# Recurrence of a decoder layer: tables of two 64x64 diagonal blocks in place of 128x128 tables

## What is computed

```
def rwkv7_scan(state0, r, w, k, v, kk, a):
    def step(S, inp):
        r_t, w_t, k_t, v_t, kk_t, a_t = inp
        sa = jnp.einsum('bhvk,bhk->bhv', S, -kk_t)
        S = (S * w_t[:, :, None, :] + sa[..., None] * (kk_t * a_t)[:, :, None, :]
             + v_t[..., None] * k_t[:, :, None, :])
        return S, jnp.einsum('bhvk,bhk->bhv', S, r_t)
    ...
    S, out = lax.scan(step, state0, xs)
```

## Time and profile before

| | us |
|---|---|
| median of 3 runs | 2958.71 (2955.7 to 2959.27) |
| the profiled execution's span | 2956.9 |
| PE busy | 2724.3 (92%) |
| DVE busy | 1186.9 (40%) |
| POOL busy | 1230.9 (42%) |
| ACT busy | 527.8 (18%) |
| PE's share of the chain of work that ended last | 87% |
| scan, first pair product to the first instruction behind it | 1169.98 to 1592.21 |

### The profile page before, as it was taken

The page is one execution under the profiler, slowest core; times in us unless marked ns, Lnnn a source line. Parts: engine busy times, 40 slices in busy tenths (PEclk is TensorE's granted clock), DMA queues, the critical chain, the costliest instruction groups (busy, mean ns, idle before and its releaser), DMA issues.

```text
span 2956.9 us, 45589 instructions
## 1 busy us (share of the span) xinstructions
PE 2724.3 (92%) x17867; PEld 2604.0 (88%) x17867; DVE 1186.9 (40%) x2064; ACT 527.8 (18%) x1098; POOL 1230.9 (42%) x949
## 2 busy tenths in 40 slices
PE   5999999999999964988888798987999999999998
PEld 5999999999999962887876398986899999999997
DVE  6332233133614359556555553153353312331333
ACT  4110011011301012332324223012121100100112
POOL 4444444444544356423332446400444444444442
PEclk8999999999999986999998699998999999999999
DMA  3111111111321100000001214222211111111111
GB/s 108 46 46 47 47 48 47 46 46 41 109 61 44 41 31 0 1 1 1 1 1 68 97 47 121 92 86 86 91 45 46 46 48 48 47 46 46 46 38 73
DMA packets 220686, 150.24 MB, mean 51 GB/s; under 512 B 10831, under 2 KB 211113, under 8 KB 219946
## 3 DMA queue, kind: packets, MB, share of 16 engines
q1 hardware_dynamic: 217850, 135.11, 15.2%
q10 hardware_dynamic: 2256, 13.71, 1.2%
q0 software_dynamic: 480, 0.05, 0.0%
HBM read 134.80 MB, written 14.04 MB: 50 GB/s over the span
## 4 chain that ended last, share of the span: by engine, by line
PE 87%; DVE 7%; ACT 2%; issue 2%; DMA 0%; POOL 0%; SPq 0%; DVEq 0%; ACTq 0%; POOLq 0%
PE bank L372 24%; PE bank L374 23%; PE bank L373 23%; PE bank L1101 3%; PE bank L1107 2%; PE bank L1094 1%; PE bank L1539 1%; PE bank L1508 1%; PE bank L1572 1%; DVE TT L1014 1%; PE bank L1161 1%; PE bank L1132 1%; PE bank L1172 1%; DVE z L829 1%; PE bank L1173 0%
## 5 line engine op out<-in xcount | busy, mean ns | idle before, releaser
L345 POOL TENSOR_TENSOR w_hi<-raw,cst 128x512 fp32r<-128x512 f32 x366 | 464.2, 1268 | 1231.5 <-PE bank L374 1051.4
L372 PE MATMUL bank<-h_hi,w_lo 128*128 128x344 f32 x2856 | 915.4, 321 | 8.9 <-issue 7.5
L374 PE MATMUL bank<-h_hi,w_hi 128*128 128x344 f32 x2856 | 914.0, 320 | 0.0
L373 PE MATMUL bank<-h_lo,w_hi 128*128 128x344 f32 x2856 | 913.4, 320 | 0.0
L372 PEld LDWEIGHTS bank<-h_hi,w_lo 128*128 128x128 f32 x2856 | 536.0, 188 | 10.9 <-issue 9.2
L350 POOL TENSOR_TENSOR w_lo<-raw,w_hi 128x512 fp32r<-128x512 f32 (+1 forms) x398 | 514.1, 1292 | 64.7 <-ACT w_hi L342 35.0
L374 PEld LDWEIGHTS bank<-h_hi,w_hi 128*128 128x128 f32 x2856 | 536.7, 188 | 1.1
L373 PEld LDWEIGHTS bank<-h_lo,w_hi 128*128 128x128 f32 x2856 | 535.0, 187 | 1.4
L374 PE MATMUL bank<-hid_hi,w_hi 128*128 128x344 f32 x1056 | 337.8, 320 | 0.0
L372 PE MATMUL bank<-hid_hi,w_lo 128*128 128x344 f32 x1056 | 337.7, 320 | 0.0
L373 PE MATMUL bank<-hid_lo,w_hi 128*128 128x344 f32 x1056 | 337.6, 320 | 0.0
(11 more groups left out here) (312 smaller groups left out, 3459.4 us busy)
## 6 DMA issues: line engine op xcount, KB each, us to landing
raw<-in_ffn_gate SPq DMA_DIRECT2D x88, 256.0 KB, 2.9
raw<-in_ffn_up SPq DMA_DIRECT2D x88, 256.0 KB, 2.9
raw<-in_ffn_down SPq DMA_DIRECT2D x80, 256.0 KB, 2.7
raw<-in_w_in SPq DMA_DIRECT2D x44, 256.0 KB, 2.8
cache<-in_cache_mem_k SPq DMA_DIRECT2D x8, 1024.0 KB, 4.9
cache<-in_cache_mem_v SPq DMA_DIRECT2D x8, 1024.0 KB, 4.9
x_save<-x ACTq DMA_DIRECT2D x1, 4128.0 KB, 12.5
x<-x_save ACTq DMA_DIRECT2D x8, 516.0 KB, 6.8
```

Source lines behind the costliest of these rows:

```text
L345: nc.gpsimd.tensor_tensor(w_hi[part], raw[part], cst[:, C_ONE:C_ONE + 1, 0:ph["width"]].to_broadcast([P, nk, ph["width"]]), ALU.mult)\
L372: nc.tensor.matmul(out, b, hi, start=first, stop=False)
L373: nc.tensor.matmul(out, a, lo, start=False, stop=False)
L374: m = nc.tensor.matmul(out, a, hi, start=False, stop=last)
```

## The change

The tables keep only the two diagonal blocks. A table of one head is now 128 partitions by 64 columns: the block of chunk 0 on partitions 0 to 63, the block of chunk 1 on 64 to 127. In detail:

- *Pair*: 32 products of 64x64 outputs and 128 columns, in place of 16 of 128 outputs and 256 columns.
- *Levels*: flip is a plain product with the identity in place of a transpose. Flip, Y and delta are each 16 products of 64x64 with 64 columns, chunk 0 and chunk 1 in turn. The tables are grouped by head parity, q = 0 and 1, four heads each: two groups in place of four. Each level has one POOL instruction for LoT in place of two, two buffers for it, and four of DVE and two of ACT in place of eight and four, of the same size each.
- TT's base is one multiplication with a mask and two additions of the identity, one per chunk, each for q = 0 and 1. MQ (MT and QKT in one) is masked in two instructions.
- *State part*: the products X, U, state and so on are issued for all heads in one go, with one eviction of 512 columns in place of two of 256. The products with MQ and LQ contract 64 rows in place of 128. Each chunk's outputs have a bank of their own.
- Bt, Kt, Vt, TT, LQ, MQ and decm have two buffers. The rounds stay in sequence on PE (`scan_tensor`).
- The next round's inputs are made inside the level loop: BK and exd between levels 0 and 1, A in level 2, R in level 3, their exponentials on ACT between its copies. rates_vector(1) moves ahead of the scan, rates_vector(2) behind the first flip of round 0.
- The mask constants are packed anew: C_PAIR holds the strict and the inclusive triangle side by side, and two levels share a table.

The core of the diff. What it leaves out are the renamed constants, the buffer addresses, and the helpers whose body is one instruction moved as it was:

```diff
...
         NLV = LEVELS - 1
...
+        B_XU, B_ST, B_OUT, B_T = 0, 1, 2, 4
...
+        def pair_tensor(pe, m):
+
+            pe.wait_ge(S("tok_ev"), 3 * m + 3)
+            pe.wait_ge(S("R_made"), m + 1)
+            for side in (0, 1):
+                for ht in range(4):
+                    for hp in (0, 1):
+                        r = rows(hp)
+                        for ck in (0, 1):
+                            t = rows(ck)
+                            i = nc.tensor.matmul(
+                                bank[B_T + 2 * side + hp][t, ht * P:(ht + 1) * P].rearrange(
+                                    "p (a t) -> p a t", a=2),
+                                BK[r, side, ht, t], AR[m % 2][r, :, ht, t], start=True, stop=True)
+                        if ht == 3:
+                            i.then_inc(S("pair"), 1)
...
+        def y_tensor(pe, m, lv):
+            pe.wait_ge(S("Loff_masked"), NLV * m + lv + 1)
+            for q in (0, 1):
+                pe.wait_ge(S("T_flip_ev"), 2 * (NLV * m + lv) + q + 1)
+                for ht in range(4):
+                    for ck in (0, 1):
+                        t = rows(ck)
+                        i = nc.tensor.matmul(y_bank(lv, q)[t, ht * CH:(ht + 1) * CH],
+                                             LoT[lv % 2][t, q, ht, :], Ti[t, q, ht, :],
+                                             start=True, stop=True)
+                i.then_inc(S("Y_t"), 1)
...
+        def x_tensor(pe, n, ck):
...
+            for ht in range(4):
+                nc.tensor.matmul(bank[B_XU][t, ht * P:(ht + 1) * P], AR[n % 2][:, 0, ht, t],
+                                 st_T[:, e % 3, ht, :], start=True, stop=False)
+                for hp in (0, 1):
+                    hc = head_cols(hp, ht)
+                    i = nc.tensor.matmul(bank[B_XU][t, hc], MQ[n % 2][t, hp, ht, 0, :], Vt[n % 2][t, hc],
+                                         start=False, stop=hp == 1)
+            i.then_inc(S("X_t"), 1)
...
+        def scan_tensor(pe):
+            for n in range(8):
+                turn_tensor(pe, n)
+                pair_tensor(pe, n)
+                for lv in range(NLV):
+                    flip_tensor(pe, n, lv)
+                    y_tensor(pe, n, lv)
+                    delta_tensor(pe, n, lv)
+                for ck in (0, 1):
+                    x_tensor(pe, n, ck)
+                    out_state_tensor(pe, n, ck)
+                    out_v_tensor(pe, n, ck)
+                    u_tensor(pe, n, ck)
+                    state_tensor(pe, n, ck)
+                    out_u_tensor(pe, n, ck)
...
+        def base_vector(dve, m, q):
+            tt = TT[m % 2][:, q]
...
+            link(nc.vector.tensor_tensor(tt, LQ[m % 2][:, q, :, 0, :],
+                                         level_mask(0).to_broadcast([P, 4, CH]), ALU.mult))
             for ck in (0, 1):
...
+                i = nc.vector.tensor_tensor(tt[t], tt[t], cst[t, C_ID:C_ID + 1, t].to_broadcast([64, 4, CH]),
+                                            ALU.add)
+            i.then_inc(S("T_base"), 1)
...
+        def scan_vector(dve):
...
+            for n in range(8):
+                tok_vector(dve, n)
+                base_vector(dve, n, 0)
+                mq_vector(dve, n)
+                base_vector(dve, n, 1)
+                flip_vector(dve, n, 0)
+                if n == 0:
+                    rates_vector(2)
+                delta_vector(dve, n, 0)
+                if n < 7:
+                    grow_vector(dve, n + 1)
+                    before_vector(dve, n + 1)
...
```

More of the change, by code:

```diff
@@ L1061, in chunk_tensor, with chunk, rows, head_cols @@
-        def chunk_tensor(pe, n):
-            mmul = nc.tensor.matmul
-            heads = lambda q: [(j, (4 * q + j) // 2, (4 * q + j) % 2) for j in range(4)]
-            pe.wait_ge(S("BK_made"), 2 * n + 2)
-            pe.wait_ge(S("out_ev"), 2 * n)
-            pe.wait_ge(S("state_add"), 4 * n)
+        B_XU, B_ST, B_OUT, B_T = 0, 1, 2, 4
+        def chunk(n):
+            return slice(n * P, (n + 1) * P)
+        def rows(ck):
+            return slice(64 * ck, 64 * ck + 64)
+        def head_cols(hp, ht):
+            return slice((2 * ht + hp) * 64, (2 * ht + hp + 1) * 64)
@@ new lines, in delta_tensor @@
+        def delta_tensor(pe, m, lv):
+            for q in (0, 1):
+                pe.wait_ge(S("Y_ev"), 2 * (NLV * m + lv) + q + 1)
+                for ht in range(4):
+                    for ck in (0, 1):
+                        t = rows(ck)
+                        i = nc.tensor.matmul(flip_bank(lv, q)[t, ht * CH:(ht + 1) * CH],
+                                             Yl[t, q, ht, :], TT[m % 2][t, q, ht, :],
+                                             start=True, stop=True)
+                i.then_inc(S("D_t"), 1)
@@ new lines, in out_state_tensor, with out_v_tensor @@
+        def out_state_tensor(pe, n, ck):
+            t, e = rows(ck), 2 * n + ck
+            pe.wait_ge(S("out_ev"), max(e - 1, 0))
+            for ht in range(4):
+                nc.tensor.matmul(bank[B_OUT + ck][:, ht * CH:(ht + 1) * CH], st_T[:, e % 3, ht, :],
+                                 AR[n % 2][:, 1, ht, t], start=ht == 0, stop=False,
+                                 skip_group_check=True)
+        def out_v_tensor(pe, n, ck):
+            t = rows(ck)
+            for ht in range(4):
+                for hp in (0, 1):
+                    nc.tensor.matmul(bank[B_OUT + ck][rows(hp), ht * CH:(ht + 1) * CH],
+                                     Vt[n % 2][t, head_cols(hp, ht)], MQ[n % 2][t, hp, ht, 1, :],
+                                     start=False, stop=False, skip_group_check=True)
@@ new lines, in out_u_tensor @@
+        def out_u_tensor(pe, n, ck):
+            t = rows(ck)
+            pe.wait_ge(S("QB_masked"), n + 1)
+            pe.wait_ge(S("U_ev"), 2 * n + ck + 1)
+            for ht in range(4):
+                for hp in (0, 1):
+                    i = nc.tensor.matmul(bank[B_OUT + ck][rows(hp), ht * CH:(ht + 1) * CH],
+                                         Us[t, head_cols(hp, ht)], LQ[n % 2][t, hp, ht, 1, :],
+                                         start=False, stop=True, skip_group_check=True)
+            i.then_inc(S("out_t"), 1)
@@ L1832, in _ @@
             g.wait_ge(S("mix_p"), 35)
-            for n in range(8):
-                chunk_pool(g, n)
+            scan_pool(g)
             sample_pool(g)
@@ L1885, in _ @@
             prep_tensor(pe)
-            for n in range(8):
-                chunk_tensor(pe, n)
+            scan_tensor(pe)
             post_tensor(pe)
@@ L1942, in _ @@
             prep_scalar(act)
-            for n in range(8):
-                chunk_scalar(act, n)
+            scan_scalar(act)
             post_scalar(act)
@@ L1988, in _ @@
             prep_vector(dve)
-            for n in range(8):
-                chunk_vector(dve, n)
+            scan_vector(dve)
             post_vector(dve)
```

536 lines of the change are left out of this document (250 added, 286 removed).

## The result

| | before | after |
|---|---|---|
| median of the runs, us | 2958.4 | 2999.47 (2998.56 to 3001.41) |
| ratio, with its 95% interval | | 1.0144 (1.013 to 1.0159) |
| span of the profiled execution, us | 2956.9 | 2997.7 |
| first X of round 0 | 1207.21 | 1198.00 |
| first X of round 7 | 1577.09 | 1608.42 |

The change makes the kernel 41 us slower, where 26 us faster was forecast. The table says where: the start of the scan is 9.2 us earlier, seven rounds take 40.5 us more, and the end, from the last round's X on, takes 25.9 us in place of 15.1. These give +42.1; what stands behind the scan is 1.3 shorter, and the span is 40.8 longer.

A forecast was written before the change was run, and what follows sets the result against it. PE bounds the recurrence's levels: 4.75 us each, no idle. A round of 49.4 against 52.84 saves 24.1 over seven, the start saves 9.0, the end loses 7.4: 25.7 saved, 2933 us, range 2891 to 2973.

The forecast's parts named there:

- the hole before the levels: Between pair and first Y, PE mostly waits while DVE works; the clock then halves for 6.8 us, adding 1.6 us.
- The clock stays low: Rival: half clock persists through three levels and the doubled state products, +15 us a round, 3050 us; chance 0.04.
- the bonus products: Four DVE products of 1.2 us in the last round, where BK stood; they cost 2.5 us.
- Diagonal tiles work at once: Level products alternating between the two diagonal 64x64 tiles overlap: 29 ns a record, 3.6 us a level.
- 5.6 for the rival: Rival: diagonal tiles take turns at 58 ns a record, 5.6 us a level, +10 a round, 3013 us; chance 0.12.
- Changes of shape: In X, each tile shape change costs 0.14 us, eight changes instead of one: +1.0, X issued in 2.8 us.
- X to X': State part, from the first chunk's X to the next X: 9.95 us, with single evictions, addition and decay of 512.
- X to pair: Whole state part, from X to the next pair: 21.2 us against 17.2, a loss of 4.0.
- pair to Y: From pair products to the first Y: 8.5 us against 10.8, or 6.3 without POOL blocking DVE.
- first level: First level, lengthened by DVE making next inputs: 5.2 us, plus 1.6 for half clock, 6.8.
- DVE beside POOL: Between pair and first Y, DVE instructions reading only SBUF stall while POOL works; without blocking 6.3 us, not 8.5.
- a second level at the low clock: Upper-bound term: half clock covers another level after the hole, +2.0 us a round.

The follow-up runs named there:

- fill_u: Changed kernel with three unread 128x128 products filling PE's wait behind U, twice a round, other waits left; 2989.4 us, ratio 1.0109.
- fill_small: Changed kernel with PE's waits behind U, behind first out_u and between turn and pair filled by unread 64x64 products; 2928.8 us, ratio 0.9899.
- xgroup: Changed kernel with X's four AR products issued before its eight MQ products, so tile shape changes twice, not eight times; 2985.3 us, ratio 1.0092.
- halves: Changed kernel with X, U and the state's change again issued, evicted, added and decayed in halves of 256 columns; 2918.4 us, ratio 0.9873.
- fill_out: Changed kernel with four unread 128x128 products behind the first chunk's out_u only; 2995.3 us, ratio 1.0131.
- xwide: Changed kernel with X's MQ products contracting all 128 rows, not 64, so rows don't change shape (output wrong); 2957.1 us, ratio 1.0003.
- before_merge: Kernel before, large tables kept, with only X, U and state's change merged to one eviction, addition and decay, out_v ahead of U; 3034.5 us, ratio 1.0256.

## Why the prediction was wrong

**The one step that failed is the clock.** The forecast had it fall once a round, in the hole before the levels, for 6.8 us. It falls earlier as well, in the state part of the first chunk, and in four of the seven rounds it stays low until past the hole: 34 us a round at the low level. The prediction had the waits that do it, "Us is one eviction of 512, 0.6, and nothing lies beside it" and the decay behind which X starts, and priced them as time only. The first of them is enough in the change; with it filled, the second does it (fill_u). The rival *The clock stays low* is the case that came. It was given 0.04, on the argument that PE would be full again at half speed. It looked at the wrong place: the levels do bring the clock back, and most of the low stretch lies ahead of them. Nor does a full PE bring it back at once: between 1206.7 and 1230.5 PE is busy for 21.25 of 23.80 us. The rival's price was +15 us a round; the whole measured excess over the forecast's round, 58.63 less 49.4, is 9.2. The 27 us added at half speed would cost half of that, 13.6, if PE alone set the pace (an estimate); the waits for DVE and ACT within them take no longer, so it is less.

Set against the sum: first X 1198.0, forecast 1198.2. Rounds 410.4, forecast 7 x 49.4 and 2.5 for the bonus products, 348.3: +62.1. End 25.9, forecast 20.0: +5.9. The first X is 0.2 early, and what stands behind the scan 1.3 shorter: the span 2997.7 is 66.5 above the forecast's 2931.2. In fill_small, where only the waits are filled, the same marks stand at 1196.5, 350.2 and 19.6 (1546.63 to 1566.27, where the scan ends), the forecast's end of the scan being 1198.2 + 348.3 + 20.0 = 1566.5. It takes 2929 us for a forecast of 2933. That two kernels of different time agree with one sum doesn't make the prediction right; it shows that the clock in the state part is the one large term at fault. That the two ends agree to 0.2 us is partly luck: the start is 1.7 us early, the rounds are 1.9 late, and the stages below are off by up to 0.4 us a round, some up and some down.

**Diagonal tiles work at once: right.** The level's period is 3.66 (1242.29 to 1245.95), forecast 3.6 and 5.6 for the rival. The rule of the Trainium skill (TensorEngine Tiling (Array Packing), Restrictions and Gotchas), which taken literally forbids the pair, is not borne out: flip, Y and delta write 64x64 tiles of different rows and columns into one bank, 32 records in 1.15 us, 0.22 of it the tail, 29 ns each. Pair even has four tiles at once, 64 records of 128 columns in 1.98 with the tail, 28 ns each; the forecast kept this as a bound.

**Changes of shape: right.** X is issued in 2.94 us (1198.00 to 1200.94), forecast 2.8; xgroup gives 0.15 for a change (14.2 us in 96, a part of them at half speed). The Trainium skill says, in the same page's Tiling Modes, that a change of mode drains TensorE; the trace agrees and prices it.

**The stages with the waits filled**, from fill_small, where the clock is low only in and behind the hole: X to X' 9.81 (forecast 9.95), X to pair 20.89 (21.2), pair to Y 8.61 (8.5), first level 6.38 (6.8), the other four to X 13.22 (12.9). In the kernel after, two of them are stretched: X to pair 28.42 (1198.00 to 1226.42) and pair to Y 9.49; the first level is 6.38 there too.

**DVE beside POOL: right.** DVE's two additions of the identity, beside two of POOL's products, timelines of DVE and POOL:

```profile
1287.11 1.82 DVE L1208 TENSOR_TENSOR TT<-TT,cst 64x256 f32<-64x256 f32 x2
...
1291.60 0.85 DVE L1208 TENSOR_TENSOR TT<-TT,cst 64x256 f32<-64x256 f32 x2
```

```profile
1287.18 2.88 POOL L1158 TENSOR_TENSOR LoT<-LQ,cst 128x512 f32<-128x512 f32 x2 [36.72 <-ACT LQ L1097]
```

1.82 for two beside POOL, 0.85 for the same two later: the term that made 8.5 of 6.3.

**The bonus products: too small.** PE waits for DVE's four products in the last round's second Y:

```profile
1593.47 1.97 PE L964 MATMUL bank<-Ti,LoT 64*64 64x64 f32 x32 [4.21 <-DVE Ti L1224]
```

In fill_small that round takes 53.2 us (1493.44 to 1546.63), forecast 49.4 + 2.5: 1.3 us too little, once.

**The range.** 2891 to 2973 took "a second level at the low clock", +2.0 a round, for its worst case. The rows had shown what an idle PE does to the clock only once a round, with a hole of 5.9 us, PE busy for 1.8 of it; that it takes a hole that large was assumed, not read. They also had the wait of 0.64 without a fall, which spoke for the assumption.

## What to carry to other kernels

A wait of PE can have two prices, its length and the clock behind it; where a change turns overlap into several short waits, put the case that the granted clock falls among the likely ones. Merging two evictions into one saves instructions and costs the overlap of the two halves: here it made PE wait, and turned a change worth 39 us (halves) into a loss of 41. When a clock is suspected, fill the waits with products that nobody reads: it tells waits from work, and may stay in the kernel if nothing better fills them.

## What the runs showed of the hardware

- The clock went to 0.50 behind a single wait of 0.68 us in the first state part (after, fill_out), and with that one filled behind one of 0.9 for the decay (fill_u). It was then low for 34 us a round, though PE's records are busy for 21.25 of the 23.80 us in the row 1206.70:1230.50 above. The Trainium skill has the gate follow how busy PE has been (TensorE: Matmul & The Clock Gate, Part 1); by the records PE was busy here, and the clock was low, so the busy share of the records doesn't foretell it. Why it stays low is open: single products of small tiles in the waits kept it up (fill_small), whole rows in X kept it up in part (xwide).
- The kernel before has waits of 0.51 and 0.64 us in its state part and stays at 1.00 there.
- A low stretch in the state part ended after 6.8 us in some places (before_merge, 1275.5 to 1282.3) and lasted 24 to 38 in the change. Both before_merge and xwide, where most were short, use all 128 rows in X; no run shows that this is the reason.
- Four 64x64 tiles work at once, at 28 ns a record of 128 columns, and two tiles in different rows and columns may write one bank at once.
- A change of tile shape costs 0.14 us at full clock and 0.19 at half. A pair of groups of X takes 0.73 and 1.23 (from 1198.00 and from 1207.82) with two changes, and 0.45 and 0.85 without them (before_merge, from 1269.77 on and from 1280.60 on).
